# Layer 1 of a two-layer decoder step keeps fourteen weight chunks between its two passes, and two row slots serve as chunk places for 166 rows

## The chip, the cores and the metric

One core of a Trainium2 chip runs the whole step. The metric is the device time of one execution in microseconds (us), the median of three runs.

## What is computed

The step is a two-layer decoder trunk in float32 on 288 tokens: 256 prompt tokens and 32 sample tokens. Layer 0 mixes tokens with a chunked gMLP, layer 1 with a short gated convolution. After each mixer comes a PEER channel mixer: every token picks 16 of 16384 experts for each of 8 heads.

```python
# layer 1's token mixer
b_gate, c_gate, h = jnp.split(x @ w_in, 3, axis=-1)
z = c_gate * h
conv = sum(conv_w[k] * zp[:, k:k + s_len] for k in range(CONV_W))
y = (b_gate * conv) @ w_out
# each layer's channel mixer
q = (xb @ w_query).reshape(PEER_BLOCK, PEER_HEADS, 2, D_HALF)
...
idx = i1 * N_KEYS + i2
u_sel = expert_u[idx]
a = jax.nn.gelu(jnp.einsum('thkd,td->thk', u_sel, xb))
return jnp.einsum('thk,thkd->td', g.astype(a.dtype) * a, expert_v[idx])
```

## The kernel before

**Rows.** The tokens lie in three tiles of 128, 128 and 32. A "row" (an entry of `ITEMS`) is one pick for each token of a tile: POOL gathers 128 expert rows of 8 KB (u and v side by side, 1 MB in all) into one of the `RING = 7` slots of `uvring` (L789). VectorE takes the dot product with the token (L1587), ScalarE makes gelu, weight and a diagonal matrix of the weights (L1177, L1185, L1189), and TensorE adds the weighted v half to the sum with that matrix (`weigh`, L841; L833 for the 32-token tile). The end of `weigh` counts `v_tensor` up, and POOL waits for it before it gathers a later row into the same slot (L788: row n waits for row n - 7). There are 576 rows: 0 to 287 in layer 0 (tile 0: 0 to 127, tile 1: 128 to 255, tile 2: 256 to 287) and 288 to 575 in layer 1 in the same way.

**Passes and chunks.** The dense work, which makes the tokens' queries, runs between the rows in four passes: each layer once for tile 0 (passes 0 and 2) and once for tiles 1 and 2 together (passes 1 and 3). Its weights come in chunks of 1 MB, loaded by SP (`load_chunk`, L723) in one order written out by hand. Layer 1 has 24 chunks: 0 to 11 for the convolution's input (`bch`, two blocks of 16 matmuls for each chunk, L852), 12 to 15 for its output (`out`, L1017), 16 to 23 for the queries (`q`, L852). Both passes of layer 1 use all 24. Pass 2 uses 0 to 19 at once, while rows 160 to 225 run; the query blocks of chunks 20 to 23 are put off (`LATE_AT`) and run inside pass 3, while rows 295 to 408 run.

**Places.** A chunk lies in one of 8 `kept` places, one `late` place in the arena, or the 3 places of `wring`. In layer 1, chunks 0, 2, 4, 6, 8, 10, 13, 15 and 18 stay in `kept` and `late` from pass 2 to pass 3. The eleven others that pass 2 uses go through `wring` and are loaded again for pass 3; chunks 20 to 23 are loaded once, in pass 3, over kept chunks 0, 2, 4 and 6 when those are used. That is 20 loads for pass 2 and 15 for pass 3.

**Order.** SP issues each load in program order. Before it issues one it waits until the last block that used the place is done (`wait_unused`, L671), and all that stands behind it waits too. `plan_steps` (L364) lays the dense steps of VectorE, ScalarE and TensorE into turns, one turn for each row: TensorE's program does the dense steps of a turn and then the turn's `weigh` (L1052 to L1059). The plan knows no load times: a block whose chunk has not landed holds TensorE, and all rows behind it. In this plan pass 2's `bch` blocks (24) stand in turns 162 to 194, its `out` steps in 197, 199, 201 and 204, its first eight query blocks in 211 to 222; pass 3's `bch` blocks stand in turns 295 to 343, its `out` steps in 351 to 360 and its queries in 380 to 405. The picks of row 288 must be ready nine rows earlier (`due`, L359).

Of the kernel before, what the change touches and what calls it, by code (L numbers as in the profile page):

```python
# [28 lines left out]
HEADS, NKEYS, TOPK = 8, 128, 16  # L29
HP = 2 * HEADS  # L30
# [42 lines left out]
def plan_homes():  # L73

    places = [("slot", s) for s in (5, 6, 2, 3, 4)] + [("ring", r) for r in range(WRING)]
    queries = [("slot", s) for s in (0, 1, 4, 5, 6)]
    home, uses, counts = [], {}, {"early": 0, "query": 0, "ring": 0}

    def take(what, of):
        counts[what] += 1
        return of[(counts[what] - 1) % len(of)]

    for n in range(PASS_CHUNK0[-1]):
        c = n - max(p for p in PASS_CHUNK0 if p <= n)
        kept = KEPT[0 if n < PASS_CHUNK0[2] else 1]
        if n >= PASS_CHUNK0[2] and c in LATE_CHUNKS:
            home.append(("kept", LATE_CHUNKS[c]))
            if n >= PASS_CHUNK0[3]:  # L90
                uses[home[-1]].append(n)
            continue
        if c in kept:
            at = ("kept", kept.index(c)) if kept.index(c) < KEEP else ("late", 0)
        elif n == PASS_CHUNK0[1]:
# [7 lines left out]
        home.append(at)  # L103
        uses.setdefault(at, []).append(n)
    return home, uses


HOME, USES = plan_homes()


def scores_of(l, t):
# [40 lines left out]
def mixer_steps(n):  # L152
# [103 lines left out]
    for c in range(4):  # L256
        for h in range(2 if l == 0 else 1):
            gated = ("gate", n, 4 * h + 3) if l == 0 else ("conv gate", n, 3)
            out.append(("PE", ("out", l, c, h, tiles[0]), row, [gated]))
            if 2 in tiles:  # L260
                out.append(("PE", ("oq", l, c, h), 0.6, [gated]))
        out.append(("DVE", ("add", l, c, tiles[0]), 0.85, [("out", l, c, 1 - l, tiles[0])]))
        for q in range(4) if n == 0 else ():
            if q == c - 1 or q == c == 3:
                quarter("ffn", q, ("add", 0, q, 0))
        if 2 in tiles:
            out.append(("ACT", ("oq read", l, c), 0.5, [("oq", l, c, 1 - l)]))
            out.append(("PE", ("of", l, c), 0.5, [("oq read", l, c)]))
            out.append(("DVE", ("add", l, c, 2), 0.85, [("of", l, c)]))
# [8 lines left out]
    if 2 in tiles:  # L278
        out.append(("ACT", ("spread", l), 3.2, [("napply", "ffn", l, 1, 1)]))
    for b in range(LATE_B if n == 2 else HP):  # L280
        out.append(("PE", ("q", n, b), blk, [("xT read", l, "ffn", tiles[-1], 1 if n else 3)]))
# [82 lines left out]
def plan_steps():  # L364
# [35 lines left out]
    def ready(e, k, behind, p):  # L400

        slow = 2 if k[0] in ("v read", "vq read", "u read", "bch read", "q read", "gate", "conv z", "conv gate") else 1
        lag = {who: 0 if who == e else slow if who == "PE" else 1 for who in ENGINES}
        if any(b not in turn or turn[b] > p - (turn[b] >= 0) * lag[by.get(b, "DVE")] for b in behind):
# [128 lines left out]
def trunk(nc, x_tok, w_chunks, rows, ln_gain, ln_bias, w_s, b_s, conv_w, conv_state, sub_keys,  # L533
          expert_uv, gains_c, ident_c, iota_c, fold_c, tril_c, smask_c, ws2_c,
          y_tok, v_rows, conv_prompt, conv_sample):
    with ExitStack() as ctx:
# [139 lines left out]

        def place_of(n):

            kind, at = HOME[n]
# [17 lines left out]

        @block.sync
        def _(sp):
            def load_chunk(n):  # L700
                l = 0 if n < PASS_CHUNK0[2] else 1
                c = n - max(p for p in PASS_CHUNK0 if p <= n)
                if c in KEPT[l] and n not in (c, PASS_CHUNK0[2] + c):
                    return
                if l == 1 and c in LATE_CHUNKS and n < PASS_CHUNK0[3]:
                    return
                if HOME[n] == ("arena", 0):

                    wait_group(sp, ("mix", 0, GROUPS - 1))
                if HOME[n] == ("late", 0):  # L710

                    wait_group(sp, ("mix", 1, GROUPS - 1))
                if HOME[n] == ("kept", 0) and l == 1:

                    wait_group(sp, ("mix", 1, GROUPS - 1))
                    sp.wait_ge(v_rows_out, 16)
                if HOME[n] in (("slot", 0), ("slot", 1)):

                    sp.wait_ge(ln_done, 2)
                if USES[HOME[n]][0] != n:  # L720
                    wait_unused(sp, USES[HOME[n]][USES[HOME[n]].index(n) - 1])
# [8 lines left out]
            for n in range(1, PASS_CHUNK0[2]):  # L730
                load_chunk(n)
# [6 lines left out]
            for n in range(PASS_CHUNK0[2], PASS_CHUNK0[3]):  # L738
                load_chunk(n)
            late_chunks = {6: (20, 21), 10: (22, 23)}  # L740
            for c in range(PASS_CHUNK0[4] - PASS_CHUNK0[3]):
                for early in late_chunks.get(c, ()):
                    load_chunk(PASS_CHUNK0[3] + early)
                if c not in LATE_CHUNKS:
                    load_chunk(PASS_CHUNK0[3] + c)
# [9 lines left out]
        def _(pool):  # L755
# [19 lines left out]
            for n, (l, t, i) in enumerate(ITEMS):  # L775
# [8 lines left out]
                if ("slot", n) in USES:  # L784
                    wait_unused(pool, USES["slot", n][-1])
                if n >= RING:

                    pool.wait_ge(v_tensor, n - RING + 1)  # L788
                pool.indirect_dma_start(  # L789
                    uvring[:, n % RING, :], None, expert_uv,  # L790
                    bass.IndirectOffsetOnAxis(ap=idx[t][:, i:i + 1], axis=0),
                ).then_inc(uv_landed[n % RING], 16)

        @block.tensor
        def _(pe):
# [9 lines left out]
            def chunk(n, c):  # L805
                m = PASS_CHUNK0[n] + c
                place, landed = place_of(m)
                if HOME[m][0] == "late":
                    loads = 1
                elif HOME[m][0] == "kept":  # L810
                    loads = 3 if n >= 2 and c in LATE_CHUNKS else n // 2 + 1
                else:
                    loads = USES[HOME[m]].index(m) + 1
                pe.wait_ge(landed, 16 * loads)
                return place

            def row_of(r, cols):
# [5 lines left out]
            def weigh(n):  # L823

                l, t, _ = ITEMS[n]
                first, last, row = n == ITEM0[l, t], n == LAST[l, t], uvring[:, n % RING, :]
# [403 lines left out]
        def _(dve):  # L1230
# [351 lines left out]

            def dot(n):
                _, t, i = ITEMS[n]
                slot, c = n % RING, n % TOPK
                dve.wait_ge(uv_landed[slot], 16 * (n // RING + 1))
# [106 lines left out]
```

## Time and profile before

| | us |
|---|---|
| median of 3 runs (lowest to highest) | 1724.96 (1724.49 to 1726.6) |
| the profiled execution | 1727.62 |
| its span, first to last instruction | 1725.8 |
| TensorE (PE) busy in the span | 1316.3 |
| VectorE (DVE) busy | 1086.5 |
| ScalarE (ACT) busy | 651.7 |
| GpSimd (POOL) busy | 632.7 |

The page of the profile gives the busy time of each engine, the span in 40 slices, the DMA queues, the chain of work that ended last, and the costliest groups. The trace behind it answers for any stretch: busy time, number of instructions (x), granted TensorE clock (1.00 is 2.4 GHz, 0.50 is 1.2 GHz), busy share of the 16 DMA engines, and the rate that they moved. The profiled execution is 1.8 us longer than its span and 2.7 us above the median.

### The profile page before, as it was taken

What the parts mean: (1) busy time and instruction counts of PE and PEld (TensorE: products, weight loads), DVE (VectorE), ACT (ScalarE), POOL (GpSimd) and SP (SyncE); (2) the same over time, 40 slices, a digit from 0 to 9 for tenths busy, and PEclk for the clock granted to TensorE, in tenths of its full rate; (3) what the DMA queues carried; (4) which work ended last, traced back from release to release, by engine and by line L of the source; (5) the groups of instructions that cost most, each with busy time, mean ns of one, the idle gap of its engine ahead of it and who ended that gap; (6) DMA issues with size and microseconds to landing.
All of it is one profiled execution on the core that took longest, in us unless ns stands there. A gap on an engine that the chain in (4) does not pass through costs nothing.

```text
span 1725.8 us, 23657 instructions
## 1 busy us (share of the span) xinstructions
PE 1316.3 (76%) x8378; PEld 631.5 (37%) x8378; DVE 1086.5 (63%) x2681; ACT 651.7 (38%) x2105; POOL 632.7 (37%) x596
## 2 busy tenths in 40 slices
PE   8998988998975678777754688797897667666744
PEld 7993545644540145433100355352462111111100
DVE  1359578555764756565676755767587666666454
ACT  2125444334433432243443423333643434434343
POOL 2014334433442433233344333434444443344341
PEclk9998999998985799997655799798897666667655
DMA  9989999999999999999999999999999999999997
GB/s 379 403 357 415 398 420 422 420 421 421 411 422 421 421 421 420 421 418 421 419 412 421 402 422 421 421 415 416 397 420 411 422 422 421 421 420 419 419 398 306
DMA packets 99382, 709.99 MB, mean 411 GB/s; under 512 B 11488, under 2 KB 11920, under 8 KB 13600
## 3 DMA queue, kind: packets, MB, share of 16 engines
q0 software_dynamic: 84192, 608.85, 85.4%
q1 hardware_dynamic: 14352, 99.16, 14.0%
q8 instruction: 66, 1.08, 0.3%
q10 hardware_dynamic: 720, 0.48, 0.1%
q14 instruction: 52, 0.43, 0.1%
HBM read 706.92 MB, written 1.52 MB: 410 GB/s over the span
## 4 chain that ended last, share of the span: by engine, by line
DMA 49%; PE 32%; ACT 7%; DVE 7%; issue 3%; POOL 2%; DVEq 0%; ACTq 0%; SPq 0%; POOLq 0%
DMA uvring<-expert_uv_dram,idx 48%; PE psum L841 12%; PE psum L852 11%; DVE uvring L1587 5%; PE psum L905 3%; PE psum L1017 3%; POOL uvring L789 2%; ACT diag L1189 1%; ACT wgt L1185 1%; ACT L1177 1%; ACT a_gelu L1177 1%; PE psum L1039 1%; PE psum L860 1%; PE psum L1000 1%; ACT L1075 1%
## 5 line engine op out<-in xcount | busy, mean ns | idle before, releaser
L1587 DVE SCALAR_TENSOR_TENSOR uvring<-uvring,xn 128x1024 f32<-128x1024 f32 x576 | 705.0, 1225 | 531.0 <-DMA uvring<-expert_uv_dram,idx 525.1
L789 POOL DMA_INDIRECT uvring<-expert_uv_dram,idx x576 | 623.9, 1083 | 1038.7 <-PE psum L841 848.8
L841 PE MATMUL psum<-uvring,diag 64*64 64x512 f32 x4096 | 686.4, 764 | 293.0 <-ACT diag L1189 280.4
L1177 ACT ACTIVATE a_gelu<-a_raw 128x1 f32<-128x1 f32 x576 | 116.6, 202 | 867.2 <-DVE uvring L1587 866.8
L841 PEld LDWEIGHTS psum<-uvring,diag 64*64 64x64 f32 x4096 | 130.7, 154 | 722.9 <-ACT diag L1189 636.6
L1189 ACT ACTIVATE diag<-twin,wgt 128x64 f32<-128x64 f32 x512 | 178.1, 348 | 48.8 <-ACT wgt L1185 1.9
L1185 ACT ACTIVATE wgt<-a_gelu,gate 128x1 f32<-128x1 f32 x576 | 169.5, 294 | 21.1 <-ACT a_gelu L1177 0.4
L833 PE MATMUL psum<-uvring,diag 128*32 128x256 f32 x512 | 67.6, 634 | 94.2 <-ACT diag L1189 83.6
L852 PEld LDWEIGHTS psum<-xT,wring 128*128 128x128 f32 x864 | 118.9, 198 | 42.0 <-issue 41.1
L852 PE MATMUL psum<-xT,wring 128*128 128x160 f32 (+1 forms) x864 | 130.3, 306 | 0.0
L852 PEld LDWEIGHTS psum<-xT,kept 128*128 128x128 f32 x896 | 115.3, 192 | 33.9 <-issue 32.3
L852 PE MATMUL psum<-xT,kept 128*128 128x160 f32 (+1 forms) x896 | 125.6, 294 | 0.0
L833 PEld LDWEIGHTS psum<-uvring,diag 128*32 128x32 f32 x512 | 13.4, 142 | 149.3 <-ACT diag L1189 135.2
L1017 PE MATMUL psum<-wring,arena 128*128 128x256 f32 x240 | 56.6, 391 | 0.0
L1068 ACT ACTIVATE arena<-psum 128x128 f32<-128x128 f32 (+2 forms) x120 | 33.9, 284 | 53.7 <-PE psum L852 46.4
L1017 PEld LDWEIGHTS psum<-wring,arena 128*128 128x128 f32 x240 | 45.5, 194 | 13.5 <-issue 7.6
L1587 DVE DVE_READ_ACCUMULATOR uvring<-uvring,xn 128x1 f32 x576 | 47.1, 82 | 0.0
L1288 DVE FIND_INDEX8 ti<-tv,scores 128x8 uint32<-128x128 f32 x144 | 38.4, 284 | 0.0
L1177 ACT ACT_TABLE_LOAD x29 | 37.2, 1283 | 0.5
L852 PE MATMUL psum<-xT,uvring 128*128 128x128 f32 x256 | 30.2, 275 | 0.7 <-ACT xT L1089 0.7
L952 PE MATMUL psum<-x,ident 64*128 64x512 f32 x48 | 26.6, 650 | 4.5 <-DVE kept L1471 4.4
L852 PEld LDWEIGHTS psum<-xT,uvring 128*128 128x128 f32 x256 | 29.3, 192 | 1.0 <-ACT xT L1089 1.0
(186 smaller groups left out, 957.3 us busy)
## 6 DMA issues: line engine op xcount, KB each, us to landing
wring<-w_chunks_dram SPq DMA_DIRECT2D x51, 1024.0 KB, 10.1
kept<-w_chunks_dram SPq DMA_DIRECT2D x20, 1024.0 KB, 14.3
uvring<-w_chunks_dram SPq DMA_DIRECT2D x17, 1024.0 KB, 17.3
uvring<-expert_uv_dram,idx POOLq DMA_INDIRECT x576, 13.4
arena<-w_chunks_dram SPq DMA_DIRECT2D x2, 1024.0 KB, 14.4
uvring<-w_chunks_dram SPq DMA_DIRECT2D x2, 512.0 KB, 7.4
uvring<-ln_gain_dram POOLq DMA_DIRECT2D x1, 1024.0 KB, 9.4
uvring<-ln_bias_dram POOLq DMA_DIRECT2D x1, 1024.0 KB, 15.0
```

The lines of the kernel that those rows point to most:

```text
L789: pool.indirect_dma_start(uvring[:, n % RING, :], None, expert_uv, bass.IndirectOffsetOnAxis(ap=idx[t][:, i:i + 1], axis=0),).then_inc(uv_ ...
L833: mm = nc.tensor.matmul(acc[32 * q:32 * q + 32, 0:256], diag[:, n % DIAGS, 0:32], row[:, D + 256 * q:D + 256 * (q + 1)], start=first, stop ...
L841: mm = nc.tensor.matmul(acc[64 * j:64 * j + 64, 512 * i:512 * (i + 1)], diag[64 * i:64 * i + 64, n % DIAGS, :], row[64 * i:64 * i + 64, D ...
L852: mm = nc.tensor.matmul(bank(key, WIDTH[n]), w[:, k, j * P:(j + 1) * P], act[:, k, 0:cols], start=(k == 0), stop=(k == KD - 1))
L905: mm = nc.tensor.matmul(bank(k, WCOLS, ROWS[t]), (xT if t else raw_T)[:, kk, 0:ROWS[t]], w[:, kk, :], start=(kk == 0), stop=(kk == KD - 1))
L1017: mm = nc.tensor.matmul(bank(key, WCOLS, ROWS[t]), act[:, h * KD + kk, LCOL[t]:LCOL[t] + ROWS[t]], w[:, kk, :], start=(h == 0 and kk == 0) ...
L1068: nc.scalar.activation(out, bank(key, n, rows), func, scale=scale).then_inc(scalar_read, 1)
L1177: nc.scalar.activation(a_gelu[:, c:c + 1], a_raw[:, c:c + 1], ACT.Gelu_apprx_tanh).then_inc(gelu_done, 1)
L1185: nc.scalar.mul(wgt[:, c:c + 1], a_gelu[:, c:c + 1], gate[t][:, i:i + 1]).then_inc(weighed, 1)
L1189: nc.scalar.mul(diag[:, n % DIAGS, 0:32 if t == 2 else 64], fold[:, :] if t == 2 else twin[:, :], wgt[:, c:c + 1]).then_inc(diag_ready, 1)
L1288: V.max_index(where[:, at:at + 8], best[:, at:at + 8], values)
L1587: nc.vector.scalar_tensor_tensor(out=uvring[:, slot, 0:D], in0=uvring[:, slot, 0:D], scalar=1.0, in1=xn[t][:, :], op0=ALU.mult, op1=ALU.mu ...
```

## The change

Layer 1 holds fourteen chunks between its passes. Ten lie in `kept` (8), `late` and one place of `wring`, two in row slots 5 and 6, and two stay in the other two places of `wring`, through which the other pass-2 chunks have gone. Rows 140 to 304 don't use slot 5, rows 141 to 306 don't use slot 6 (`AWAY`); a row takes the slot, of those there are, that was used longest ago (`plan_rows`). When a held chunk is used in pass 3, its place takes one of the ten chunks that pass 3 still has to load (`AGAIN`: 20 to 23, then 12 to 17). Pass 2 has 20 loads as before, pass 3 has 10.

SP's order is now: chunks 2 to 11, then 0 and 1 (each waits for the last row of its slot, 138 and 139), then 12 to 19 through two places of `wring`, then the ten. Chunks 14 to 19 each wait for the use of the chunk two before them. The planner has a new kind of condition (`lands`): pass 2's `out` steps from the third on, and its query blocks, stand at least six turns after the step that frees their chunk's place.

```diff
-KEPT = [(1, 5, 9, 12, 14, 29, 30, 31), (0, 2, 4, 6, 8, 10, 13, 15, 18)]
+KEPT = (1, 5, 9, 12, 14, 29, 30, 31)
+HELD = {2: ("kept", 1), 3: ("kept", 2), 4: ("kept", 3), 5: ("kept", 4), 6: ("kept", 0), 7: ("late", 0),
+        8: ("kept", 5), 9: ("kept", 6), 10: ("kept", 7), 11: ("ring", 2), 0: ("slot", 5), 1: ("slot", 6)}
+PASSED = {c: ("ring", c % 2) for c in range(12, 20)}
+AGAIN = dict(zip(LATE + list(range(12, 18)), (HELD[c] for c in range(2, 12))))
+AWAY = {5: (140, 305), 6: (141, 307)}
...
+    for c, at in [*HELD.items(), *PASSED.items()]:
+        loads.append((at, [second + c] + [third + c] * (c not in AGAIN)))
+    for c, at in AGAIN.items():
+        loads.append((at, [second + c] * (c in LATE) + [third + c]))
...
+        s = min((s for s in range(RING) if s not in AWAY or not AWAY[s][0] <= n < AWAY[s][1]),
+                key=lambda s: latest.get(s, s - RING))
...
-            out.append(("PE", ("out", l, c, h, tiles[0]), row, [gated]))
+            passed = [("lands", ("out", 1, c - 2, 0, 0), 6)] if n == 2 and c >= 2 else []
+            out.append(("PE", ("out", l, c, h, tiles[0]), row, [gated, *passed]))
...
+            passed = [("lands", ("out", 1, 2 + b // 2, 0, 0) if b < 4 else ("q", 2, b // 2 * 2 - 3), 6)]
...
+                if at[0] == "slot" and l == 1:
+
+                    sp.wait_ge(v_tensor, max(m for m in range(AWAY[at[1]][0]) if SLOT[m] == at[1]) + 1)
+                if BEFORE[n] is not None:
+                    wait_unused(sp, BEFORE[n])
...
-                if n >= RING:
-
-                    pool.wait_ge(v_tensor, n - RING + 1)
+                if n in ROW_AFTER:
+                    wait_unused(pool, ROW_AFTER[n])
+                if ROW_BEFORE[n] is not None:
+
+                    pool.wait_ge(v_tensor, ROW_BEFORE[n] + 1)
```

## Rows read from the trace of the kernel before

**Rows 1.** The page, the span in 40 slices: DMA busy share, rate.

```profile
DMA  9989999999999999999999999999999999999997
GB/s 379 403 357 415 398 420 422 420 421 421 411 422 421 421 421 420 421 418 421 419 412 421 402 422 421 421 415 416 397 420 411 422 422 421 421 420 419 419 398 306
```

**Rows 2.** The page, the chain that ended last, by engine.

```profile
DMA 49%; PE 32%; ACT 7%; DVE 7%; issue 3%; POOL 2%; DVEq 0%; ACTq 0%; SPq 0%; POOLq 0%
```

**Rows 3.** The page, DMA issues: count, size, median us to landing.

```profile
wring<-w_chunks_dram SPq DMA_DIRECT2D x51, 1024.0 KB, 10.1
uvring<-expert_uv_dram,idx POOLq DMA_INDIRECT x576, 13.4
```

**Rows 4.** Dot products of 815 to 862 and 597.5 to 615 us: count, durations, first, last.

```profile
L1587 DVE SCALAR_TENSOR_TENSOR uvring<-uvring,xn x20: 1218/1225/1227, 814.3 to 861.5; 128x1024 f32<-128x1024 f32 x20
L1587 DVE SCALAR_TENSOR_TENSOR uvring<-uvring,xn x7: 1215/1226/1298, 597.8 to 612.7; 128x1024 f32<-128x1024 f32 x7
```

**Rows 5.** Busy time by stretch: PE, PEld, DVE, ACT, POOL, clock, DMA share, GB/s.

```profile
489.00:547.00 58.00, 31.57 (x184) 8.67 (x180) 28.11 (x67) 14.53 (x49) 17.04 (x17) 0.65 1.01 421
547.00:603.00 56.00, 37.00 (x188) 7.56 (x192) 38.74 (x94) 25.62 (x78) 22.27 (x22) 0.67 1.01 421
603.00:708.00 105.00, 85.30 (x649) 53.73 (x642) 62.96 (x167) 32.40 (x114) 34.69 (x34) 0.95 1.01 421
762.00:799.00 37.00, 31.78 (x236) 18.22 (x234) 21.64 (x64) 12.77 (x48) 15.11 (x14) 0.91 1.01 420
978.00:1012.00 34.00, 34.00 (x255) 22.87 (x254) 21.10 (x56) 14.48 (x48) 15.78 (x14) 1.00 1.00 405
1012.00:1094.00 82.00, 69.25 (x486) 44.83 (x484) 46.79 (x134) 24.05 (x88) 25.58 (x25) 0.94 1.01 421
1120.00:1175.00 55.00, 51.45 (x366) 30.17 (x363) 36.04 (x110) 18.23 (x65) 19.37 (x20) 0.97 1.01 414
```

**Rows 6.** SP's queue in order of time: start, us, loads.

```profile
495.59 1.52 SPq L723 DMA_DIRECT2D kept<-w_chunks_dram  x1
...
499.53 0.43 SPq L723 DMA_DIRECT2D kept<-w_chunks_dram  x1
615.86 0.33 SPq L723 DMA_DIRECT2D wring<-w_chunks_dram  x1
...
687.56 0.42 SPq L723 DMA_DIRECT2D kept<-w_chunks_dram  x1
...
731.64 63.10 SPq L723 DMA_DIRECT2D wring<-w_chunks_dram  x4
986.46 15.55 SPq L723 DMA_DIRECT2D kept<-w_chunks_dram  x2
...
1041.20 126.61 SPq L723 DMA_DIRECT2D wring<-w_chunks_dram  x6
```

**Rows 7.** PE in order of time, pass 2: start, us, instructions.

```profile
656.91 2.05 PE L852 MATMUL psum<-xT,kept 128*128 128x128 f32 x16
658.89 1.95 PE L841 MATMUL psum<-uvring,diag 64*64 64x512 f32 x16
660.77 2.05 PE L852 MATMUL psum<-xT,kept 128*128 128x128 f32 x16
```

**Rows 8.** One row from its dot product to the next gather, all engines.

```profile
793.47 1.23 DVE L1587 SCALAR_TENSOR_TENSOR uvring<-uvring,xn 128x1024 f32<-128x1024 f32 x1 [1.25 <-DMA uvring<-expert_uv_dram,idx]
...
795.36 0.35 ACT L1189 ACTIVATE diag<-twin,wgt 128x64 f32<-128x64 f32 x1
...
795.76 1.09 PE L841 MATMUL psum<-uvring,diag 64*64 64x512 f32 x8 [0.36 <-ACT diag L1189]
...
797.49 0.94 POOL L789 DMA_INDIRECT uvring<-expert_uv_dram,idx  x1 [0.85 <-PE psum L841]
```

**Rows 9.** Row 7, an early row: its gather, its dot product.

```profile
133.31 1.18 POOL L789 DMA_INDIRECT uvring<-expert_uv_dram,idx  x1 [9.94 <-PE psum L841]
...
140.25 1.23 DVE L1587 SCALAR_TENSOR_TENSOR uvring<-uvring,xn 128x1024 f32<-128x1024 f32 x1
```

**Rows 10.** Rows 256 and 257, the first of tile 2: weighing, next gather.

```profile
885.53 1.94 PE L833 MATMUL psum<-uvring,diag 128*32 128x256 f32 x16 [5.77 <-DVE x L1607]
...
886.92 0.94 POOL L789 DMA_INDIRECT uvring<-expert_uv_dram,idx  x1 [5.58 <-PE psum L833]
```

More of the change, by code:

```diff
@@ L78, in plan_homes @@
     queries = [("slot", s) for s in (0, 1, 4, 5, 6)]
-    home, uses, counts = [], {}, {"early": 0, "query": 0, "ring": 0}
+    loads, counts = [], {"early": 0, "query": 0, "ring": 0}
     def take(what, of):
@@ L83, in take @@
         return of[(counts[what] - 1) % len(of)]
-    for n in range(PASS_CHUNK0[-1]):
+    for n in range(PASS_CHUNK0[2]):
         c = n - max(p for p in PASS_CHUNK0 if p <= n)
[L87 to L91, printed above, removed]
+        if c in KEPT:
+            if n == c:
+                loads.append((("kept", KEPT.index(c)), [c, PASS_CHUNK0[1] + c]))
             continue
-        if c in kept:
-            at = ("kept", kept.index(c)) if kept.index(c) < KEEP else ("late", 0)
-        elif n == PASS_CHUNK0[1]:
+        if n == PASS_CHUNK0[1]:
             at = ("arena", 0)
@@ L102, in plan_homes, with plan_rows @@
             at = take("ring", [("ring", r) for r in range(WRING)])
[L103 to L108, printed above, removed]
+        loads.append((at, [n]))
+    second, third = PASS_CHUNK0[2], PASS_CHUNK0[3]
+    for c, at in [*HELD.items(), *PASSED.items()]:
+        loads.append((at, [second + c] + [third + c] * (c not in AGAIN)))
+    for c, at in AGAIN.items():
+        loads.append((at, [second + c] * (c in LATE) + [third + c]))
+    home, before, last = {}, {}, {}
+    for at, users in loads:
+        count, previous = last.get(at, (0, None))
+        last[at] = count + 1, users[-1]
+        before[users[0]] = previous
+        for n in users:
+            home[n] = at, count + 1
+    return loads, home, before
+LOADS, HOME, BEFORE = plan_homes()
+def plan_rows():
+    slot, count, before, after, latest = [], [], [], {}, {}
+    for n in range(len(ITEMS)):
+        s = min((s for s in range(RING) if s not in AWAY or not AWAY[s][0] <= n < AWAY[s][1]),
+                key=lambda s: latest.get(s, s - RING))
+        rows = [m for m in range(n) if slot[m] == s]
+        chunks = [users[-1] for at, users in LOADS if at == ("slot", s) and (users[0] >= PASS_CHUNK0[2]) == bool(rows)]
+        if not rows or s in AWAY and rows[-1] < AWAY[s][0] <= n:
+            after[n] = chunks[-1]
+        slot.append(s)
+        count.append(len(rows) + 1)
+        before.append(rows[-1] if rows else None)
+        latest[s] = n
+    return slot, count, before, after
+SLOT, ROW_COUNT, ROW_BEFORE, ROW_AFTER = plan_rows()
 def scores_of(l, t):
@@ L280, in mixer_steps @@
     for b in range(LATE_B if n == 2 else HP):
-        out.append(("PE", ("q", n, b), blk, [("xT read", l, "ffn", tiles[-1], 1 if n else 3)]))
+        passed = []
+        if n == 2:
+            passed = [("lands", ("out", 1, 2 + b // 2, 0, 0) if b < 4 else ("q", 2, b // 2 * 2 - 3), 6)]
+        out.append(("PE", ("q", n, b), blk, [("xT read", l, "ffn", tiles[-1], 1 if n else 3), *passed]))
         out.append(("ACT", ("q read", n, b), 0.35, [("q", n, b)]))
@@ L403, in ready @@
         lag = {who: 0 if who == e else slow if who == "PE" else 1 for who in ENGINES}
-        if any(b not in turn or turn[b] > p - (turn[b] >= 0) * lag[by.get(b, "DVE")] for b in behind):
+        if any(b[1] not in turn or turn[b[1]] > p - b[2] for b in behind if b[0] == "lands"):
+            return False
+        if any(b not in turn or turn[b] > p - (turn[b] >= 0) * lag[by.get(b, "DVE")]
+               for b in behind if b[0] != "lands"):
             return False
@@ L699, in _, with load_chunk @@
         def _(sp):
-            def load_chunk(n):
+            def load_chunk(at, n):
                 l = 0 if n < PASS_CHUNK0[2] else 1
                 c = n - max(p for p in PASS_CHUNK0 if p <= n)
[L703 to L707, printed above, removed]
+                if at == ("arena", 0):
                     wait_group(sp, ("mix", 0, GROUPS - 1))
-                if HOME[n] == ("late", 0):
+                if at == ("late", 0):
                     wait_group(sp, ("mix", 1, GROUPS - 1))
-                if HOME[n] == ("kept", 0) and l == 1:
+                if at == ("kept", 0) and l == 1:
                     wait_group(sp, ("mix", 1, GROUPS - 1))
                     sp.wait_ge(v_rows_out, 16)
-                if HOME[n] in (("slot", 0), ("slot", 1)):
+                if at in (("slot", 0), ("slot", 1)):
                     sp.wait_ge(ln_done, 2)
-                if USES[HOME[n]][0] != n:
-                    wait_unused(sp, USES[HOME[n]][USES[HOME[n]].index(n) - 1])
+                if at[0] == "slot" and l == 1:
+                    sp.wait_ge(v_tensor, max(m for m in range(AWAY[at[1]][0]) if SLOT[m] == at[1]) + 1)
+                if BEFORE[n] is not None:
+                    wait_unused(sp, BEFORE[n])
                 place, landed = place_of(n)
@@ L729, in _ @@
                 sp.dma_start(place[:, half, :], w_chunks[0][:, half, :]).then_inc(done, 16)
-            for n in range(1, PASS_CHUNK0[2]):
-                load_chunk(n)
+            first = [(at, users[0]) for at, users in LOADS if users[0] < PASS_CHUNK0[2]]
+            for at, n in first[1:]:
+                load_chunk(at, n)
                 if 18 <= n < 20:
@@ L737, in _ @@
             sp.dma_start(keys[:, :, :], sub_keys[1]).then_inc(keys_landed, 16)
[L738 to L745, printed above, removed]
+            for at, users in LOADS[len(first):]:
+                load_chunk(at, users[0])
             for t in range(2):
@@ L807, in chunk @@
                 place, landed = place_of(m)
[L808 to L814, printed above, removed]
+                pe.wait_ge(landed, 16 * HOME[m][1])
                 return place
@@ L825, in weigh @@
                 l, t, _ = ITEMS[n]
-                first, last, row = n == ITEM0[l, t], n == LAST[l, t], uvring[:, n % RING, :]
+                first, last, row = n == ITEM0[l, t], n == LAST[l, t], uvring[:, SLOT[n], :]
                 if first and n:
@@ L1584, in dot @@
                 _, t, i = ITEMS[n]
-                slot, c = n % RING, n % TOPK
-                dve.wait_ge(uv_landed[slot], 16 * (n // RING + 1))
+                slot, c = SLOT[n], n % TOPK
+                dve.wait_ge(uv_landed[slot], 16 * ROW_COUNT[n])
                 nc.vector.scalar_tensor_tensor(
```

12 lines of the change are left out of this document (5 added, 7 removed).

## The prediction

> **What bounds the kernel.** I read the rate by slices first, then the chain that ended last, then stretches. The 16 DMA engines are busy in nearly every slice and stand at 419 to 422 GB/s over most of the span [rows 1]; the chain that ended last lies 49% in DMA [rows 2]. A stretch with rows alone gives the price of a row: 20 dot products start between 814.3 and 861.5 us, 19 steps of 2.48 us [rows 4]. A chunk is as large as a row (1 MB, 1.0486 million bytes), so at 421 GB/s a load costs 2.49 us. The sum of both must explain a stretch: 489 to 547 us holds 15 rows (the 17 in its row are gathers issued) and eight loads (seven chunks, first and last shown, and the keys) [rows 5, 6]: 15 x 2.48 + 8 x 2.49 = 57.1 of 58 us. 603 to 708 us holds 33 rows and nine loads [rows 5, 6]: 81.8 + 22.4 = 104.2 of 105 us. So in these stretches bytes set the time. Two stretches differ: in 978 to 1012 us TensorE is busy 34.00 of 34 us and the rate falls to 405; in 1120 to 1175 us it is busy 51.45 of 55 at 414 [rows 5]. There a load is nearly free already.
>
> One rule speaks of this rate. The Trainium skill ("DMA: Bandwidth & Descriptors", section "Where 436 GB/s comes from") says that loads from HBM are bound at about 358 GB/s for a core; by it a load would cost 2.93 us, an estimate, and five 14.6. The trace shows 421 and decides.
>
> **Part 1, five loads fewer.** 35 loads of layer 1 become 30: 5 x 2.49 = 12.4 us, if each was on the path. They don't vanish from one place, so I count loads by stretch, before and after, from SP's queue [rows 6] and the order in the diff.
> - Rows 125 to 162: keys and 7 chunks become keys and 14 (2 to 11, 0, 1, 12, 13). DMA sets the pace at both times: +7 loads, +17.4 us. Chunks 0 and 1 now wait on SP for rows 138 and 139 to be weighed; behind them stand only 12 and 13. Chunk 0 is wanted in turn 162, some 20 rows or 50 us later, against 10.1 us to land [rows 3]. I cost the wait at nothing; without that cover TensorE would wait for the landing.
> - Rows 162 to 195 (603 to 708 us): nine loads become none, -22.4 us. Can TensorE follow at 2.48 us a row? Back to back a block takes 658.89 - 656.91 = 1.98 us and two weighings 660.77 - 658.89 = 1.88 us [rows 7]; 24 blocks and 33 weighings are 47.5 + 31.0 = 78.5 us, under the 81.8 of the rows. From 597.8 to 612.7 us, where blocks run already and no load has been issued yet, seven dots come 2.48 us apart [rows 4, 6]. But TensorE was busy 85.30 us of this stretch [rows 5], part of it at a clock below 1.00. What I lose is between 0 (rows 4) and 6 us (85.30 plus 2 to 3 us of waiting, against 81.8); I take 2, nearer to the row that shows the pace itself.
> - Rows 195 to 212: four loads (16 to 19 before, 14 to 17 after): 0.
> - Rows 212 to 257: of the four loads that begin at 731.64, the last three (chunks 1, 3 and 5 for pass 3) lie here [rows 6]; after, 18 and 19. TensorE is busy 31.78 of 37 us [rows 5], but the six-turn gaps spread the query blocks: -2.5 us.
> - Rows 295 to 342: nine loads from 986.46 on [rows 6]; after, 20 to 23 and 12 to 16, nine too. But the first moves from row 298 to 302, because its place is now freed by chunk 2 and not by chunk 0. It leaves the stretch that TensorE bounds and comes back in one at 421 GB/s (1012 to 1094 us) [rows 5]. Between 0 and +2.5 us; I take +1.5, since part of it still falls before 1012.
> - Rows 342 to 361: three loads (the last of the six from 1041.20 on) [rows 6] become one: 5.0 us less to move, but TensorE idles only 3.5 of 55 us [rows 5]. Between -3.5 and -1; I take -3.
>
> Sum: 17.4 - 22.4 + 2 - 2.5 + 1.5 - 3 = -7.0 us.
>
> **Part 2, five slots for rows 145 to 305.** A slot must go round in 5 x 2.48 = 12.4 us instead of 17.4, or the DMA engines run dry. The round has two halves. From the dot's start to the next gather: 793.47 to the end of weighing at 796.85 is 3.4 us, to POOL's start at 797.49 4.0 us [rows 8]; at the low clock weighing takes up to a microsecond more. From the gather's start to the dot: usually 13.4 us to landing [rows 3], but that is queueing behind other rows. Its floor is POOL's 0.94 us and the row's own 2.48: 3.4 us. Its ceiling is row 7, which started with few rows ahead and still came behind them: 140.25 - 133.31 = 6.9 us [rows 9]. So the round needs between 7.4 and 11.9 us, under 12.4 at both ends; I take 9 to 10, and a slot can be 2.5 us late before it costs anything. It is later than that where a tile begins: TensorE waits 5.77 us for the sum of the last tile to be read, and POOL 5.58 us for TensorE [rows 10]. Two such places (rows 256 and 288) lie in the range, and the second runs into the TensorE-bound stretch. By the floor that is 0, by the ceiling some 2 us for each and 1 us of smaller ones: 0 to 5; I take +1.
>
> **Part 3, the rest.** The six-turn gaps move pass 2's third `out` step from turn 201 to 203 and the end of the queries by about three turns. Row 288's picks are due at turn 279: hidden by 50 rows. The new waits on POOL (rows 305 and 307, for blocks in turns 296 and 299) stand before all later gathers, but are over when rows 300 and 302 are weighed: 0. The loads that pass 3 now has are issued when their place is freed (turns 302 to 343) and used from 317 on, 15 turns later at least: 0.
>
> **Forecast.** -7.0 + 1 = -6.0 us: the profiled span would go from 1725.8 to 1719.8, and the median from 1724.96 to 1719.0 us; the profiled execution stands 2.7 us above the median, which I take as the same after. All gains and no losses would be 1712.6.
>
> **Rivals.**
> - The gain goes to TensorE. With the loads gone from rows 162 to 195, TensorE is the bound there: 85.30 us busy plus waits, 88 instead of 84; in rows 295 to 361 the full 2.5 us are pushed on and only 1 us is saved. The sum is 17.4 - 22.4 + 6 - 2.5 + 2.5 - 1 + 1 = +1: 1723 to 1727. For it: 51.45 of 55 and 34.00 of 34 us busy [rows 5]. Against it: the seven dots at 2.48 us [rows 4].
> - Five slots starve the DMA engines: slower. If the round takes longer than 12.4 us on the common row, each row without a load beside it loses a fifth of the excess. There are some 120 such rows (145 to 197 and 225 to 295), so 0.25 us of excess takes the forecast's 6 us and 0.6 us gives 1719 + 14 = 1733. It decides where landing from an idle queue takes over 8 us, against 6.9 at most in rows 9. A rule speaks for it: the same page of the Trainium skill ("Latency and other measured facts") gives HBM access 0.2 us on average and 2 us at high load. No run here shows a gather with five slots; by that rule, as an estimate, 9.5 us become some 11.5, still inside 12.4, with the late rows costing the 5 us of the upper end.
> - Two passing places are too few: chunks 14 to 19 have six turns, 15 to 20 us, to land. The median is 10.1 us [rows 3]. If one lands late, TensorE holds all rows: up to 2 us for each of six, 1720 to 1730.
>
> **Chances.** Forecast 0.57 (own range 1713 to 1721.5), TensorE 0.21, starving 0.15, passing places 0.07. The range 1713.5 to 1727 leaves out the starved case and a sliver below. About 0.2% (3.5 us) is what a measurement of this kernel can tell from no change. Faster by more: the forecast and a little of the others, 0.60; within: 0.25; slower: 0.15.
>
> **What would show it.** Right: 30 layer-1 loads in SP's queue; a rate of 421 in rows 125 to 147, which take 17 us longer; rows 162 to 195 in 82 to 86 us with TensorE above 90% busy; 2.48 us between dots in rows 225 to 255. Wrong: dots more than 2.55 us apart there with a rate below 415 (starving), TensorE near 100% busy with VectorE's dots waiting for nothing in rows 162 to 195 (TensorE), or an idle TensorE before an `out` or query block with rows ready (passing places).

## The result and the profile after

The changed kernel is slower: 1731.18 us (1729.06 to 1736.12) against 1723.85 us, a ratio of 1.0039 (95% interval 1.0030 to 1.0048), +7.3 us where 6 us less were forecast. The profiled executions stand above their medians, 1736.12 after (the slowest of nine) and 1727.62 before, and their spans differ by 8.5 us (1734.3 and 1725.8). Stages below come from these two traces, each from the start of one row's dot product to that of another.

From the page of the changed kernel: busy share of the DMA engines and rate in 40 slices, the chain that ended last, and two groups of DMA issues.

```profile
DMA  9989999999999999999999999999999999999997
GB/s 383 404 364 412 406 420 421 421 421 421 407 422 421 402 400 367 410 416 395 385 374 416 384 410 421 420 417 390 421 420 421 421 422 421 422 420 419 421 405 310
...
DMA 48%; PE 34%; DVE 8%; ACT 6%; issue 3%; POOL 1%; DVEq 0%; ACTq 0%; SPq 0%; POOLq 0%
...
wring<-w_chunks_dram SPq DMA_DIRECT2D x39, 1024.0 KB, 9.8
...
uvring<-expert_uv_dram,idx POOLq DMA_INDIRECT x576, 12.6
```

Against [rows 1] the rate has a hole in the 14th to the 23rd slice (564 to 997 us): 367 to 416 GB/s where it was 402 to 421. That is rows 142 to 297, the rows of five slots. Yet the busy share still reads 9: in rows 162 to 195 below, the share is 0.97 at 382 GB/s, since a slow packet counts as busy too. The rate, not the share, shows the loss. The loads did fall, from 51 to 39 through `wring` [rows 3], with seven more into other places: five in all. So fewer bytes moved, and more slowly.

Stretches of the changed kernel, between the dot products of rows 125 and 145, 162 and 195, 212 and 257, 257 and 295, 342 and 361. The columns are those of [rows 5].

```profile
487.84:576.26 88.42, 41.26 (x224) 10.21 (x220) 35.91 (x83) 21.60 (x69) 20.30 (x20) 0.59 1.01 421
619.48:710.56 91.08, 85.11 (x656) 53.69 (x652) 63.77 (x168) 33.30 (x116) 36.93 (x34) 0.96 0.97 382
764.00:887.94 123.94, 86.72 (x504) 30.27 (x500) 75.75 (x191) 43.22 (x151) 49.94 (x45) 0.75 0.99 397
887.94:990.11 102.17, 44.92 (x324) 9.97 (x328) 71.84 (x167) 41.83 (x131) 40.00 (x39) 0.55 0.96 386
1132.36:1185.19 52.83, 49.47 (x356) 28.94 (x356) 36.53 (x109) 17.61 (x66) 19.00 (x19) 0.94 0.99 403
```

The same rows in the kernel before, rows 212 to 257 and 257 to 295:

```profile
761.54:881.35 119.81, 89.85 (x500) 29.03 (x498) 75.63 (x192) 43.21 (x151) 47.95 (x46) 0.73 1.01 420
881.35:978.11 96.76, 43.65 (x305) 9.50 (x306) 71.73 (x168) 40.43 (x126) 38.42 (x37) 0.52 1.01 414
```

In rows 212 to 295 every engine does the same work within 4 us, and no engine is near the length of the stretch, but the rate fell from 420 and 414 to 397 and 386. That points at gathers that are issued too late; the experiments test it. Stage by stage, in us:

| rows | before | after | difference | forecast |
|---|---|---|---|---|
| up to 125 | 489.1 | 487.8 | -1.2 | 0 |
| 125 to 162 | 113.7 | 131.6 | +17.9 | +17.4 |
| 162 to 195 | 105.4 | 91.1 | **-14.3** | -20.4 |
| 195 to 212 | 53.3 | 53.4 | +0.1 | 0 |
| 212 to 257 | 119.8 | 123.9 | **+4.1** | -2.5 |
| 257 to 295 | 96.8 | 102.2 | **+5.4** | 0 |
| 295 to 342 | 141.5 | 142.2 | +0.8 | +1.5 |
| 342 to 361 | 55.5 | 52.8 | -2.7 | -3 |
| 361 to the last dot | 542.3 | 540.7 | -1.6 | 0 |

Three stages miss by 6.1, 6.6 and 5.4 us, 18.1 together; Part 2 had set +1 aside for all of them. All three lie where two slots are missing. In the 45 steps of rows 212 to 257 the median is 2.49 us in both kernels; 9 steps are over 2.9 us after, 5 before. So the common row keeps its pace, and late rows pay.

One late row of the changed kernel, all engines in order of time (start, us, what; in brackets the idle time before it and what ended it):

```profile
838.79 4.47 PE L870 MATMUL psum<-uvring,diag 64*64 64x512 f32 x24 [2.74 <-ACT diag L1218]
...
841.08 1.97 POOL L824 DMA_INDIRECT uvring<-expert_uv_dram,idx  x1 [3.01 <-PE psum L870]
...
845.16 1.23 DVE L1616 SCALAR_TENSOR_TENSOR uvring<-uvring,xn 128x1024 f32<-128x1024 f32 x1 [1.62 <-DMA uvring<-expert_uv_dram,idx]
...
850.00 1.23 DVE L1616 SCALAR_TENSOR_TENSOR uvring<-uvring,xn 128x1024 f32<-128x1024 f32 x1 [1.95 <-DMA uvring<-expert_uv_dram,idx]
```

POOL waited 3 us for weighing, then took 1.97 us for a gather that usually takes 0.94. The gather was out at 843.05, 2.1 us before the row ahead of it was ready (845.16), and its own dot started 6.95 us later, 4.84 us after the one ahead instead of 2.48.

### The profile page after: what moved, and what is told of

Its sections match the earlier page's. It is cut to its first block, busy times and chain, and to the rows that moved or that the text cites. A ratio compares the mean times of both kernels' runs of the same rounds, so it can differ in the third digit from the quotient of the medians.

```text
span 1734.3 us, 23657 instructions
## 1 busy us (share of the span) xinstructions
PE 1313.0 (76%) x8378; PEld 634.0 (37%) x8378; DVE 1087.3 (63%) x2681; ACT 651.2 (38%) x2105; POOL 649.2 (37%) x596
## 4 chain that ended last, share of the span: by engine, by line
DMA 48%; PE 34%; DVE 8%; ACT 6%; issue 3%; POOL 1%; DVEq 0%; ACTq 0%; SPq 0%; POOLq 0%
DMA uvring<-expert_uv_dram,idx 47%; PE psum L870 12%; PE psum L881 11%; DVE uvring L1616 6%; PE psum L1046 4%; PE psum L934 3%; ACT diag L1218 1%; ACT wgt L1214 1%; POOL uvring L824 1%; ACT a_gelu L1206 1%; PE psum L1068 1%; PE psum L889 1%; ACT L1206 1%; PE psum L862 1%; PE psum L1029 1%
## 5 line engine op out<-in xcount | busy, mean ns | idle before, releaser
L824 POOL DMA_INDIRECT uvring<-expert_uv_dram,idx x576 | 640.4, 1112 | 1031.8 <-PE psum L870 835.4
L881 PEld LDWEIGHTS psum<-xT,kept 128*128 128x128 f32 x1056 | 138.7, 194 | 42.2 <-issue 42.2
L881 PE MATMUL psum<-xT,kept 128*128 128x160 f32 (+1 forms) x1056 | 151.3, 298 | 0.0
L881 PEld LDWEIGHTS psum<-xT,wring 128*128 128x128 f32 x544 | 74.6, 194 | 23.2 <-issue 22.4
L881 PE MATMUL psum<-xT,wring 128*128 128x160 f32 (+1 forms) x544 | 81.5, 305 | 0.6 <-DVE arena L1569 0.6
L1097 ACT ACTIVATE arena<-psum 128x128 f32<-128x128 f32 (+2 forms) x120 | 33.9, 284 | 52.6 <-PE psum L881 45.8
L881 PE MATMUL psum<-xT,uvring 128*128 128x128 f32 (+1 forms) x384 | 48.1, 281 | 0.7 <-ACT xT L1118 0.7
L881 PEld LDWEIGHTS psum<-xT,uvring 128*128 128x128 f32 x384 | 45.5, 191 | 7.4 <-issue 5.7
L1580 DVE TENSOR_TENSOR x<-x,psum 128x256 f32<-128x256 f32 (+1 forms) x24 | 9.9, 412 | 37.0 <-PE psum L1046 37.0
```

The source lines that it names most:

```text
L824: pool.indirect_dma_start(uvring[:, SLOT[n], :], None, expert_uv, bass.IndirectOffsetOnAxis(ap=idx[t][:, i:i + 1], axis=0),).then_inc(uv_l ...
L881: mm = nc.tensor.matmul(bank(key, WIDTH[n]), w[:, k, j * P:(j + 1) * P], act[:, k, 0:cols], start=(k == 0), stop=(k == KD - 1))
L1097: nc.scalar.activation(out, bank(key, n, rows), func, scale=scale).then_inc(scalar_read, 1)
```

## The experiments

Two theories stood at first. **A**: five slots are too short a queue; that alone costs what the change lost. **B**: the loss comes from the moved loads and blocks (TensorE, passing places), not from the slots. Ratios are to the kernel before on the same chip.

**Five slots alone.** The kernel before, with only the slots taken away.

```diff
+AWAY = {5: (140, 305), 6: (141, 307)}
+SLOT, ROW_COUNT, ROW_BEFORE = plan_rows()
...
-                    pool.wait_ge(v_tensor, n - RING + 1)
+                    pool.wait_ge(v_tensor, ROW_BEFORE[n] + 1)
```

> The kernel before with all its 35 layer-1 loads and its order of loads; only slots 5 and 6 stay unused from row 140 (141) to 304 (306). Theory A (short queue): with five slots the DMA engines run dry at each small delay; the loads of rows 165 to 224 cover that there, rows 225 to 305 have no cover and lose what the changed kernel lost there, 3.4 + 3.5 + 0.5 + 1.5 us, with 0 to 5 us more before: 1731 to 1738 us. Theory B (moved loads): five slots cost next to nothing, as predicted (0 to 5 us), and what the change lost lies in where the loads stand: 1723 to 1727 us.

Measured: 1741.12 us, ratio 1.0088 (1.0074 to 1.0102), +15 to 16 us. Rows 212 to 257 take 128.1 instead of 119.8 us, rows 257 to 295 101.9 instead of 96.8:

```profile
767.21:895.26 128.05, 91.32 (x512) 31.23 (x508) 75.73 (x191) 43.26 (x151) 48.84 (x47) 0.72 0.99 400
895.26:997.12 101.86, 45.46 (x324) 10.36 (x328) 71.84 (x167) 41.70 (x130) 38.94 (x38) 0.53 0.96 385
```

The slots alone cost more than the change lost, 3 us more than A's upper end; B falls.

**The load order alone.** The change's order with all seven slots; chunks 0 and 1 go through two places of `wring` and are loaded again, as are chunks 18 and 19 (34 loads).

```diff
-AWAY = {5: (140, 305), 6: (141, 307)}
+AWAY = {}
...
+    for c in (0, 1):
+        loads.append((("ring", c), [second + c]))
```

> The changed kernel's order of loads with all seven slots for rows: chunks 0, 1, 18 and 19 go through the two passing places and are loaded again, so 34 loads, one fewer than before; 12 of them stand before row 150. Theory A: with seven slots nothing runs dry, rows 162 to 195 take 84 to 90 us where the kernel before took 105.4, and the total is 1719 to 1724 us. Theory B: with the loads gone from rows 162 to 195 these take 90 us or more and the total is 1728 us or more.

Measured: 1723.99 us, ratio 0.9995 (0.9986 to 1.0004). That is in A's range at its upper end, and rows 162 to 195 take 88.1 us, as A expected. One load fewer would be 2.5 us; about 1 shows. So the order itself costs some 1.5 us, and about 3 at the end of the interval.

**Six slots alone.** The kernel before without slot 6 only.

```diff
+AWAY = {6: (141, 307)}
```

> The kernel before with its 35 loads and their order; slot 6 alone stays unused in rows 141 to 306, so six slots. Five slots cost 16 us in this form. If the price is one of delays that exceed a fixed slack, a sixth slot adds 2.5 us of slack and most delays fit: 0 to 4 us, 1724 to 1729 us. If each slot less costs about the same, 8 us: 1731 to 1735 us.

Measured: 1725.06 us, ratio 1.0001 (0.9992 to 1.0010). Going from seven to six costs nothing, from six to five 15 us: an edge, not a slope.

**Six slots in the change.** Chunk 0 stays in slot 5; slot 6 keeps its rows, and chunk 1 passes through `wring` and is loaded again, as is chunk 19 (32 loads).

```diff
-        8: ("kept", 5), 9: ("kept", 6), 10: ("kept", 7), 11: ("ring", 2), 0: ("slot", 5), 1: ("slot", 6)}
+        8: ("kept", 5), 9: ("kept", 6), 10: ("kept", 7), 11: ("ring", 2), 0: ("slot", 5)}
-AWAY = {5: (140, 305), 6: (141, 307)}
+AWAY = {5: (140, 305)}
```

> The changed kernel with one row slot given away instead of two: chunk 0 in slot 5, chunk 1 through a passing place and loaded again, chunk 19 too: 32 loads, six slots for rows 140 to 304. Theory A: a slot has 14.9 us to go round instead of 12.4, and most delays fit: three loads save 7.5 us, six slots cost 2 to 6: 1718 to 1723 us. Theory B: 1727 to 1732 us.

Measured: 1719.25 us (1717.02 to 1720.13), ratio 0.9965 (0.9953 to 0.9977): 6 us faster than the kernel before, as A expected. Its rows 162 to 195, 212 to 257 and 257 to 295:

```profile
615.03:701.87 86.84, 83.48 (x656) 53.22 (x653) 63.24 (x168) 32.69 (x115) 39.19 (x34) 0.97 1.00 411
754.26:873.94 119.68, 87.55 (x508) 29.82 (x500) 75.62 (x193) 43.21 (x151) 47.48 (x46) 0.77 1.01 420
873.94:970.89 96.95, 44.08 (x320) 9.81 (x320) 71.80 (x168) 40.42 (x126) 38.32 (x38) 0.53 1.01 411
```

The first holds one load: 86.84 - 2.49 = 84.4 us for 33 rows, against 84 that the prediction gave them (81.8 + 2). The other two are back at the lengths of before.

**Six slots, then five for 22 rows.** As above, with chunk 1 in slot 6 from row 284 on (31 loads).

```diff
-AWAY = {5: (140, 305)}
+AWAY = {5: (140, 305), 6: (284, 307)}
```

> The kernel with six slots and 32 loads (1719.25 us), with slot 6 given to chunk 1 for pass 3 in rows 284 to 306 alone, and chunk 19 kept in its passing place: 31 loads. One load less saves 2.5 us; five slots for 22 rows, across a change of layer, cost 1.5 us as they did in rows 288 to 295 of the changed kernel, or up to 4: 1717 to 1721 us.

Measured: 1719.75 us, ratio 0.9964 (0.9952 to 0.9976), no different from six slots with 32 loads. Rows 257 to 295 take 101.2 us instead of 97.0. Of these 4.2 us, 2.5 are chunk 1's second load, which now stands there and not in rows 212 to 225 (rows 212 to 257 fall from 119.7 to 117.3); some 1.8 us are left for the five slots, most of the load saved.

**What makes a round of five slots too long?** Three cuts, each in the changed kernel, each taking one delay out of the half of the round that isn't DMA. The first computes pass 2's `bch` blocks over 2 of 8 parts of the sum; the second leaves out half of each weighing in rows 140 to 304; the third computes other gates, with a function that needs fewer switches of ScalarE's table (rows 212 to 257 have no table load instead of two).

```diff
+                depth = 2 if name == "bch" and n == 2 else KD
-                for k in range(KD):
+                for k in range(depth):
```

> The changed kernel; the 24 convolution blocks of pass 2 multiply a quarter of their depth (2 of 8 steps), so that TensorE is nearly free in rows 162 to 195. The changed kernel took 91.1 us there against 82 us of bytes. If the delays that five slots don't forgive come from TensorE running late, these rows fall to 82 to 85 us and the total from 1731 to 1723 to 1726 us. If they come from the gathers themselves (the last of 16 engines landing late, a slow gather instruction), these rows stay at 88 to 91 us and the total at 1728 to 1731 us.

Measured: 1726.34 us, ratio 1.0008 (0.9997 to 1.0019), just above the first expectation. Rows 162 to 195 fall from 91.1 to 83.5 us, inside it (in the fastest of eleven executions, 1722.96 us):

```profile
619.30:702.83 83.53, 55.00 (x372) 20.75 (x375) 63.37 (x169) 32.93 (x115) 36.20 (x34) 0.96 1.01 414
```

With six slots the full blocks fit into 84.4 us. So TensorE could nearly follow, and most of what the blocks cost there is lateness that five slots don't absorb.

```diff
-                    for q in range(4):
+                    for q in range(2 if 140 <= n < 305 and not (first or last) else 4):
...
-                    for c in range(2):
+                    for c in range(1 if 140 <= n < 305 and not (first or last) else 2):
```

> The changed kernel; rows 140 to 304 (not the first or last of a tile) do half of the weighing's matmuls, so a slot comes free 0.5 us sooner at the full clock and 1.0 us at the half, and TensorE has 16 us less to do in rows 162 to 195. If the five slots lose by the time round the slot, the loss in rows 225 to 305 halves and that in rows 162 to 195 goes: 1720 to 1725 us against 1731. If the gathers' own delays set it, whatever stands behind them: 1728 to 1731 us.

Measured: 1726.61 us, ratio 1.0010 (1.0002 to 1.0019), between the two expectations. Rows 225 to 257 fall from 86.0 to 81.2 us, rows 257 to 288 from 82.9 only to 81.4.

```diff
-                        nc.scalar.activation(gate[t][:, c], gate[t][:, c], ACT.Exp, accum_out=esum[t][:, h:h + 1]
+                        nc.scalar.activation(gate[t][:, c], gate[t][:, c], ACT.Copy, accum_out=esum[t][:, h:h + 1]
```

> The changed kernel; the softmax's exponential is replaced by a copy (the gates have other values), so that ScalarE needn't change its table between a gelu and an exponential; rows like 159, 175, 237 and 268, whose weights come 1.3 to 1.8 us late, should be gone. If such single delays are what five slots don't forgive, 3 to 6 us less than the changed kernel: 1725 to 1728 us. If they fit into the slack: 1730 to 1732 us.

Measured: 1726.83 us (1719.56 to 1735.60), ratio 1.0007 (0.9994 to 1.0020): a wide spread, but under the changed kernel and inside the first expectation. Rows 225 to 257 take 81.2 us, rows 257 to 288 81.8.

**All three cuts, and a control.** The three diffs above in the changed kernel, and the same three in the kernel before.

> The changed kernel with three cuts at once, each of which alone took 4.4 to 4.9 us off it: pass 2's bch blocks with 2 of their 8 matmuls, half of the weighing's matmuls in rows 140 to 304, and the gates through Copy instead of Exp, so that ScalarE switches tables less. It leaves out part of the dense sums and of the weighing and computes other gates. Theory P (the price of five slots is made up of delays in the half of the loop that isn't DMA: TensorE late, weighing long, ScalarE late; each adds): ratio to the kernel before about 0.9955 to 0.9975, -4 to -8 us, and rows 212 to 257 within 1 us of 112 + 2 loads x 2.49 = 117 us. Theory Q (a gather's landing alone, with its last engine late, breaks a loop of five slots): the three cuts overlap, and it stays at 0.999 to 1.001; rows 212 to 257 at 119 us or more.

> The control: the kernel before with the same three cuts, leaving out the same parts of the computation. With seven slots a slot has 17.4 us to go round, so delays of some us cost nothing, and most stretches are bound by bytes: theory P expects 0.9985 to 1.0, of which the part under 1 comes from rows 288 to 306 and 342 to 361, where TensorE was busy most; if it falls by as much as the changed kernel with the cuts does (over 6 us), the cuts act on something that both kernels share and say nothing of five slots.

Measured: 1723.06 us, ratio 0.9983 (0.9974 to 0.9993), and 1725.53 us, 1.0003 (0.9993 to 1.0013), for the control. With seven slots the cuts bring nothing, with five 8 to 10 us: they act through the round. But 0.9983 lies between what theories P and Q expected, and in the trace, the slowest of ten executions (1726.21 us), rows 212 to 257 and 257 to 295 did not come back: 122.4 us and 102.0 us.

```profile
756.63:878.99 122.36, 91.27 (x332) 32.68 (x328) 75.88 (x192) 40.66 (x149) 46.70 (x45) 0.74 0.99 400
878.99:980.94 101.95, 45.35 (x182) 9.88 (x184) 71.85 (x168) 38.84 (x128) 41.86 (x37) 0.53 0.97 391
```

So single delays are part of the price, 8 to 10 us when all three go at once. Each alone brought 4 to 5, so they overlap and don't add as P had it. A part remains without them: 1723.06 us is still 3 to 4 us above the six-slot kernel, which has two loads more.

**The round by itself.** Left was whether a gather's landing can come down, when it must, to what a nearly idle queue gives (4.5 us). Rows 430 to 531 of the kernel before have no load and no dense block beside them; there it was run with five slots and with four. With four, four times the step of a row is the round.

```diff
+AWAY = {5: (430, 531), 6: (431, 532)}
```

> The kernel before with slots 5 and 6 unused in rows 430 to 531, where nothing but rows runs: no load, no dense block, no clock change. The half of a round that isn't DMA takes 2.3 (dot to weighing) + 1.1 to 2.0 (weighing, by the clock) + 0.4 + 0.94 (POOL), 4.7 to 5.6 us. Theory R (a gather issued behind others lands no sooner than 6.5 to 7 us after POOL is done, so that a round needs 11.5 to 12.5 us and five slots have nothing over at the low clock): rows 435 to 528 come 2.58 to 2.70 us apart instead of 2.525, +5 to +16 us in all. Theory S (landing can come down to the 4.5 us of an idle queue, and the price of five slots comes from TensorE blocks, loads and tile starts beside the rows): 2.52 to 2.55, 0 to +2 us.

```diff
+AWAY = {4: (429, 530), 5: (430, 531), 6: (431, 532)}
```

> As five_late with slot 4 unused too: four slots for rows 430 to 531. Four times the step of a row is then the round itself, so the step measures it. Theory R: (4.7 to 5.6 + 6.5 to 7)/4 = 2.8 to 3.15 us a row, rows 435 to 528 in 260 to 293 us against 234.8, +26 to +58 us. Theory S: (4.7 to 5.6 + 4.5)/4 = 2.3 to 2.5, so the rate of the DMA engines still sets the step, 2.53 to 2.65 us, +1 to +12 us.

Measured: 1730.55 and 1773.74 us in one execution each, beside 1725.22. The 91 rows from 435 to 526 in the kernel before, with five and with four slots:

```profile
1362.90:1593.12 230.22, 152.55 (x736) 25.01 (x728) 154.86 (x372) 89.06 (x295) 92.17 (x91) 0.67 1.01 421
```

```profile
1359.07:1596.18 237.11, 154.65 (x736) 25.61 (x728) 154.92 (x372) 89.11 (x295) 93.45 (x92) 0.65 1.00 405
```

```profile
1364.45:1638.33 273.88, 168.93 (x728) 26.73 (x728) 154.85 (x371) 89.34 (x295) 90.77 (x91) 0.56 0.95 352
```

That is 2.53, 2.61 and 3.01 us a row. In the traces of all twelve kernels with seven slots there, the 91 rows take 230.1 to 230.3 us, so the 6.9 us between the first two are clear of noise. Theory R asked for 2.58 to 2.70 and 2.80 to 3.15, S for at most 2.55 and 2.65: S falls. Five slots cost even where nothing but rows runs, and four slots show a round of 12.0 us in which landing took 6.5 on average, not 4.5.

One round with five slots, from the five-slot trace (the dot at 1491.11 is that of the row ahead):

```profile
1485.75 0.94 POOL L807 DMA_INDIRECT uvring<-expert_uv_dram,idx  x1 [1.55 <-PE psum L859]
...
1491.11 1.23 DVE L1605 SCALAR_TENSOR_TENSOR uvring<-uvring,xn 128x1024 f32<-128x1024 f32 x1 [0.59 <-DMA uvring<-expert_uv_dram,idx]
...
1493.59 1.23 DVE L1605 SCALAR_TENSOR_TENSOR uvring<-uvring,xn 128x1024 f32<-128x1024 f32 x1 [1.25 <-DMA uvring<-expert_uv_dram,idx]
...
1495.48 0.35 ACT L1207 ACTIVATE diag<-twin,wgt 128x64 f32<-128x64 f32 x1
...
1495.88 1.96 PE L859 MATMUL psum<-uvring,diag 64*64 64x512 f32 x8 [1.39 <-ACT diag L1207]
...
1498.13 0.94 POOL L807 DMA_INDIRECT uvring<-expert_uv_dram,idx  x1 [2.04 <-PE psum L859]
```

Gather 0.94, landing 6.90 (1486.69 to 1493.59), dot to weighing 2.29, weighing 1.96, to the next gather 0.29: 12.4 us. Five slots at 2.48 us a row have 12.4 us, and this round, with no delay in it, fills them. In the same stretch some weighings take 1.09 us, and then there is 0.9 us more to spare: the stretch holds both of TensorE's clock levels (0.65 granted on average), so the "no clock change" of the expectation doesn't hold.

The common row still keeps the pace: the median step is 2.48 us with five slots and 2.49 with seven. Late rows cost: 13 of the 91 steps are over 2.9 us with five slots, 5 with seven, and together they are 11.0 and 4.1 us over 2.48 us a step. The difference of 6.9 us is that of the whole stretch. With four slots the median itself is 2.78 us.

Can landing be shorter when needed? For each row I took the lead, from the end of its gather on POOL to the dot of the row ahead (how early the gather is out before the row ahead is ready), and the mean step between the two dots: rows 165 to 193, 226 to 253 and 259 to 283 of the changed kernel, and 435 to 525 with five and with four slots, 264 rows.

```
lead, us      rows   end of gather to dot   step from the row ahead
0.5 to 2.5      24          5.34                  3.38
2.5 to 3.5      43          6.33                  3.24
3.5 to 4.5      70          6.83                  2.68
4.5 to 6.0     103          7.77                  2.57
over 6.0        24          9.34                  2.46
```

The third column is the lead plus the last column. A gather that is out less than 3.5 us before the row ahead is ready loses 0.8 to 0.9 us against 2.48; from 3.5 us on it loses 0.2 or less. In the round above the lead was 4.42 us (1486.69 to 1491.11), so some 0.9 us of it could have been given up. With seven slots all 91 rows of the stretch lead by over 6 us. That is the edge: at the low clock six slots leave at least 14.9 - 12.4 = 2.5 us for delays, five leave 0 to 0.9.

## Why the prediction was wrong

**The failing step is Part 2.** It gave a round 9 to 10 us, so that a slot could be 2.5 us late, and found two places later than that: +1 us, at most 5. The slots alone cost 15 to 16 us, and three of the stages that they touch missed by 18 us. The term that was mis-sized is the slack of a slot: 0 to 0.9 us at the low clock. The kind of price was right: late rows pay it, but many and not two.

- From the dot to the next gather I had 3.4 to 4.0 us from [rows 8], and "up to a microsecond more" at the low clock, which went into the upper bound of 11.9 us but not into the 9 to 10. At 1.96 us of weighing it is 4.5 us, inside those bounds, and rows 212 to 295 stand partly at the low clock (0.75 and 0.55 granted on average).
- From the gather's start to the dot I took a floor of 3.4 us (POOL and the row's own bytes) and row 7's 6.9 us as a ceiling [rows 9]. The round above takes 0.94 + 6.90 = 7.8 us, above the ceiling; with a lead of only 3.5 us, the edge of the table, I estimate 0.94 + 3.5 + 2.48 = 6.9 us, the ceiling itself. 3.4 never shows: even with the row ahead nearly in, a row's dot starts 4.4 us after POOL is done at the earliest. Row 7 was no ceiling: its lead was only 3.1 us, under the edge of 3.5 (its gather was out at 133.31 + 1.18 = 134.49, and the row ahead was ready at 137.57):

```profile
137.57 1.23 DVE L1587 SCALAR_TENSOR_TENSOR uvring<-uvring,xn 128x1024 f32<-128x1024 f32 x1 [0.32 <-DMA uvring<-expert_uv_dram,idx]
```

- I called 12.4 minus 9 or 10 "2.5 us late before it costs anything". There is 0.9 us at most at the low clock. A row that is later than that costs time, and so do delays that seven slots hide: weighing behind a block, a table switch, a gather of 1.97 us.

**The rival was right, its turning point and its common row wrong.** "Five slots starve the DMA engines", at 0.15, said slower, near 1733, against 1731.18. It said 0.6 us of excess on 120 rows gives that; rows 225 to 257 came 2.69 us apart on average, with 397 GB/s in rows 212 to 257, past both marks (2.55 us, 415) named as its sign. But it let every common row pay, and the common row keeps the step that it had before (2.49 us in rows 212 to 257); that its sum came so near is in part luck. And it was to decide "where landing from an idle queue takes over 8 us". That is not what decides: with at most the row ahead in the queue landing takes 4.4 to 4.7 us. What decides is landing in the flow plus the rest of the round, 11.5 to 12.4 us against five steps of 2.48, and the delays that come on top.

**Part 1 held.** Rows 125 to 162: +17.4 forecast, +17.9 found. Rows 195 to 212: 0 and +0.1. Rows 295 to 342: +1.5 and +0.8; 342 to 361: -3 and -2.7. Rows 162 to 195 and 212 to 257 missed in the changed kernel, but with six slots they came to 84.4 us without a load, and 119.7 with three loads, as many as before; with two loads (the 31-load kernel) rows 212 to 257 take 117.3. So bytes by stretch was a sound account. The rate of [rows 4] was read where seven slots feed it, and Part 1 took it over into rows of five; that is Part 2's error again.

**TensorE as the bound** (0.21, 1723 to 1727) was not what made rows 162 to 195 long: with six slots they come to 84.4 us without their load, where the rival said 88, though TensorE was busy 83.5 of 86.8 us. Its lateness cost mostly through the round. Rows 295 to 306 don't speak against it: the load order alone ran these 11 rows in 27.8 us instead of 33.9, with TensorE busy throughout both times (34.00 of 34 us before [rows 5]):

```profile
971.62:999.43 27.81, 27.81 (x211) 18.52 (x213) 20.88 (x56) 14.38 (x48) 11.94 (x11) 1.00 0.99 394
```

That is 211 matmuls instead of 255, at 0.13 us each in both. So TensorE may have been the bound there both times, with less work in the shorter stretch, and only one load is issued in it instead of four. Which of the two gave the 6 us was not tried.

**Passing places** (0.07): rows 195 to 225, where chunks 14 to 19 pass through, took 91.3 us against 90.5 before, and the trace has no wait of TensorE for a load there: no sign of it.

Part 3 was right as far as it shows: rows from 361 on are 1.6 us shorter.

What stays open: why a gather that is out late comes 0.8 to 0.9 us more than a step behind the row ahead. Of the 6.3 us that it takes from POOL's end at a lead of 3.1, the lead and one step of 2.48 make up 5.6. The Trainium skill ("DMA: Bandwidth & Descriptors", section "Latency and other measured facts") gives HBM access 0.2 us on average and 2 us at high load. The 0.8 to 0.9 us lie between, but no run shows where in the DMA path they are spent.

## What to carry to other kernels

Before taking a buffer from a ring, write out one full round with durations at the lower clock, and take the landing from rows in a flow as dense as the new one, not from an early or an idle one; then compare it with (slots) x (step). If the rest is under a few of the delays that the trace shows, each of them becomes time. And try one buffer less before two: here giving up the seventh slot cost nothing, and the change with that slot alone won 6 us where giving two lost 7.

## What the runs showed of the hardware

- The step of the flow depends on how early the next gather is out, with an edge near 3.5 us of lead; in rows 435 to 526 four slots in flight reach 352 GB/s, five 405, seven 421.
- A row is ready with the last of 16 engines, which can be far behind: in the late row above, 15 engines were done 4.52 us after POOL, the last 6.94.
- In the rows of five slots more packets are slow: of the 8 KB packets in rows 162 to 195, 188 of 4240 took over 0.45 us, against 8 of 5406 before (0.31 us is usual); in rows 212 to 257 175 of 6003 against 17 of 6131. Whether a gap in the flow causes it isn't shown.
- A gather's time on POOL is not fixed. In rows 226 to 257 it took from 0.94 us to 1.97:

```profile
L824 POOL DMA_INDIRECT uvring<-expert_uv_dram,idx x32: 936/938/1965, 802.5 to 887.3; - x32
...
DMA to landing us min/median/max: 7.8/8.6/11.2
```

The same rows of the kernel before have such gathers too, so they aren't due to the change:

```profile
L789 POOL DMA_INDIRECT uvring<-expert_uv_dram,idx x32: 936/936/1951, 799.7 to 880.4; - x32
...
DMA to landing us min/median/max: 11.2/12.8/16.4
```

The landing, from the gather's start, has a median of 8.6 us after, against 12.8 before: the shorter queue shows first in this number.
